# A two-layer hybrid decoder on one core: the opening re-ordered around the raw memory tokens, and the second mixer's end cut into parts

## Chip, cores, metric

One NeuronCore of a Trainium2 chip runs one Bass program (hand-written instruction streams for the five engines, tied together by semaphores). The metric is device time in microseconds of the core. Median before: 1234.83 us of 3 runs (1234.59 to 1236.22).

## The reference, cut to what matters

512 tokens of width 1024 go through two layers; float32 throughout. Each layer adds a mixer, cross attention to 256 memory tokens, and a sparse mixture of experts.

```python
mkv = rmsnorm(mem, mem_norm_g) @ w_mem_kv          # 256x1024 @ 1024x2048, once for both layers
xn  = rmsnorm(h, norm_mix_g[0])                    # layer 0, even mixer: gated MLP half and S5 half
z   = xn @ w_in                                    # 1024 -> 1536; the last 512 columns feed the S5
# S5: lam_bar = exp(lam*step); b_bar = ((lam_bar-1)/lam)*B; a linear scan; y = Re(C x) + D u
# layer 1, odd mixer: z = rmsnorm(h) @ w_in (1024 -> 3592)
hh = rmsnorm(mlstm(q, k, v, i, f), hn_g) * sigmoid(c_o)    # yc, 4 heads
yd = block-sparse causal attention, 4 heads                 # "sparse head" below
h  = h + concatenate([yc, yd]) @ w_out                      # 1024 -> 1024
```

## The kernel before, in words

Matrices live in SBUF as 128-partition blocks; x as four token tiles of 128, transposed into eight blocks of 128 columns. Weights come as panels of 2 MB (all 1024 rows, 512 columns) into two slots W0 and W1 in turn. SP issues each panel when the last result of the slot's previous panel has been filled (`load_panel`, L545).

Two kinds of product. The memory's four panels kv0 to kv3 are plain float32 products (`memory_gemm`, L871; each is two token tiles by eight blocks, and each matmul leaves two records). All layer products are split (`split_gemm`, L813 to L840): for each of the eight steps k, ACT copies the weights' block into a rounded high part (`weights`, L1435), GpSimd subtracts it for the low part (`low_parts`, L674), and TensorE makes three passes for each of four banks (L835). High and low parts have a ring of four. x is split in the same way, ACT the high part (`high_part`, L1427), VectorE the low part (`low_part`, L1933).

PSUM's eight banks go round by a written list (`uses_of_banks`): each use claims its bank when the use before has been copied out. In layer 1 two groups of four banks, G and O, turn separately; the sparse heads' scores (`ms`), turned probabilities (`mt`) and turned gated blocks (`ycT`) share O. The order of work on each engine is the order of the program.

**The opening, before.** SP: memory tokens, the S5 loads (small pieces, L603), kv0 and kv1, x (four quarters, L607), a second copy of B (L610), fifteen small loads (L612), then kv2 and so on. ACT's queue loads the rows of gains; GpSimd's the S5 rows (L649), then it makes the constants, the identity among them, and reports all at once. TensorE turns the gains and S5 rows (`cols`, L849), then the memory, which ACT has squared, and VectorE scaled by its reciprocal root (L1984); VectorE copies the turned blocks times the gain (L1989, L1990). TensorE: kv0, the turned C (`ct`, L882), kv1, kv2, the turned B tables (`bT`, L892), x turned (`mix_norm0`, L813), kv3, the first split panel ev2 (L835), the table product w (L906). VectorE between: S5 angles (L1998 to L2016), powers (from L2019), B and C (to L2038), x's root, ten steps of `combine` for the B tables, x scaled (L2055), nine `combine` for the C powers with x's low parts between (L2044 to L2046). ACT: squares and root of the memory, exponentials and sines (L1504 to L1513), squares of x (L1458) and its root (L1463).

**The second mixer's end, before.** After the last projection (dv, panel od6) TensorE turns the probabilities of sparse head 1 (`moba_turn`, L1368), multiplies head 0 (`moba_out`, L1379), makes head 3's scores (`moba_scores`, L1357), multiplies head 1, turns head 2, turns the gated blocks (L1400), and runs the output panel out10, with the rest of heads 2 and 3 between its steps. VectorE finds each row's maximum (L2585 to L2587), scales the probabilities by the reciprocal sum (`moba_probs`, L2593, L2594), and copies every second bank (L2600); ACT makes the exponentials (L1854) and the other copies (L1862). For the mLSTM half, GpSimd squares all 2048 columns (L765), VectorE sums (L2626), ACT takes the root (L1892), VectorE the reciprocal (L2630), and GpSimd multiplies by it (L768) and by the gate (L769), each in one piece; only then does it make the output panel's low parts. ACT makes that panel's high parts behind head 3's exponentials.

## Time and profile before

| | us |
|---|---|
| median of 3 runs | 1234.83 |
| the profiled execution | 1233.99 |
| its span | 1232.2 |
| TensorE matmul busy | 1163.9 (94%) |
| weight load | 863.5 (70%) |
| VectorE | 716.7 (58%) |
| ScalarE (ACT) | 588.2 (48%) |
| GpSimd (POOL) | 357.5 (29%) |
| DMA, mean over the span | 174 GB/s |
| mean granted TensorE clock | 0.983 of full |

The profile is one execution; its times run from the span's start. "Idle before, releaser" is how long an engine stood still before an instruction and what ended that. Matmul ends are modelled and overlap, so the distance of two starts is their cost. The two stretches that the change touches are 0 to about 122 us and about 795 to 858 us.

### The profile page before, as it was taken

What the parts mean: (1) busy time and instruction counts of PE and PEld (TensorE: products, weight loads), DVE (VectorE), ACT (ScalarE), POOL (GpSimd) and SP (SyncE); (2) the same over time, 40 slices, a digit from 0 to 9 for tenths busy, and PEclk for the clock granted to TensorE, in tenths of its full rate; (3) what the DMA queues carried; (4) which work ended last, traced back from release to release, by engine and by line L of the source; (5) the groups of instructions that cost most, each with busy time, mean ns of one, the idle gap of its engine ahead of it and who ended that gap; (6) DMA issues with size and microseconds to landing.
All of it is one profiled execution on the core that took longest, in us unless ns stands there. A gap on an engine that the chain in (4) does not pass through costs nothing.

```text
span 1232.2 us, 15359 instructions
## 1 busy us (share of the span) xinstructions
PE 1163.9 (94%) x5227; PEld 863.5 (70%) x5227; DVE 716.7 (58%) x1294; ACT 588.2 (48%) x1130; POOL 357.5 (29%) x311
## 2 busy tenths in 40 slices
PE   4999999999999799999899999979999997999996
PEld 2458876788777566666678877757887774666665
DVE  5893443322332688888745992772223326888887
ACT  2453245445634266665535354352465343666661
POOL 2024350564222021113136663253342220211130
PEclk9999999999999899999899999999999998999999
DMA  9532331278102799997232130012321017999963
GB/s 279 150 106 99 40 111 69 70 289 323 69 1 96 299 391 368 391 376 293 72 126 77 69 136 1 2 68 69 137 69 69 1 67 318 380 375 390 379 228 125
DMA packets 77643, 214.92 MB, mean 174 GB/s; under 512 B 23620, under 2 KB 24560, under 8 KB 65272
## 3 DMA queue, kind: packets, MB, share of 16 engines
q1 hardware_dynamic: 64688, 180.22, 39.7%
q0 software_dynamic: 10048, 28.92, 6.4%
q10 hardware_dynamic: 2840, 4.91, 1.1%
q8 instruction: 40, 0.66, 0.2%
q14 instruction: 27, 0.22, 0.1%
HBM read 187.90 MB, written 32.51 MB: 179 GB/s over the span
## 4 chain that ended last, share of the span: by engine, by line
PE 83%; DVE 9%; ACT 3%; issue 2%; DMA 1%; POOL 1%; DVEq 0%; POOLq 0%; ACTq 0%
PE bank L835 39%; PE bank L1183 7%; PE bank L1216 7%; PE bank L1188 6%; PE bank L871 5%; PE bank L1053 2%; PE bank L1075 2%; PE bank L1129 2%; DMA E<-xs,idx 1%; DVE h L2412 1%; PE bank L1102 1%; PE bank L1014 1%; DVE E2r L2373 1%; PE bank L1239 1%; ACT E2r L1736 1%
## 5 line engine op out<-in xcount | busy, mean ns | idle before, releaser
L674 POOL TENSOR_TENSOR wlo<-W,whi 128x512 fp32r<-128x512 f32 x176 | 254.6, 1458 | 451.6 <-ACT whi L1435 431.5
L1435 ACT ACTIVATE whi<-W 128x512 fp32r<-128x512 f32 x176 | 108.1, 633 | 238.4 <-PE bank L835 231.8
L835 PE MATMUL bank<-whi,xTr 128*128 128x512 f32 x480 | 193.1, 402 | 0.9 <-ACT E L1878 0.7
L835 PE MATMUL bank<-wlo,xTr 128*128 128x512 f32 x416 | 162.5, 391 | 0.0
L835 PEld LDWEIGHTS bank<-whi,xTr 128*128 128x128 f32 x480 | 90.6, 189 | 21.8 <-POOL wlo L674 1.7
L835 PE MATMUL bank<-whi,E4r 128*128 128x512 f32 x256 | 99.8, 390 | 0.0
L1188 PE MATMUL bank<-E4r,E1r 128*128 128x512 f32 x360 | 98.5, 422 | 0.0
L1216 PE MATMUL bank<-whi,E2r 128*128 128x512 f32 x256 | 91.2, 418 | 6.7 <-DVE E2r L2373 5.2
L835 PEld LDWEIGHTS bank<-wlo,xTr 128*128 128x128 f32 x416 | 78.6, 189 | 16.6 <-issue 1.2
L1973 DVE TENSOR_TENSOR h<-bank,h 128x512 f32<-128x512 f32 x32 | 21.8, 692 | 115.0 <-PE bank L835 115.0
L1188 PEld LDWEIGHTS bank<-E4r,E1r 128*128 128x128 f32 x360 | 67.6, 188 | 27.0 <-issue 7.4
L707 POOL COPY idx<-slots 128x1 uint32 (+1 forms) x30 | 5.5, 182 | 276.5 <-PE bank L1163 186.0
L1216 PEld LDWEIGHTS bank<-whi,E2r 128*128 128x128 f32 x256 | 49.8, 195 | 24.4 <-DVE E2r L2373 14.2
L835 PE MATMUL bank<-whi,E0r 128*128 128x512 f32 x160 | 63.7, 398 | 0.0
L835 PE MATMUL bank<-whi,E2r 128*128 128x512 f32 x160 | 62.4, 390 | 0.0
L835 PE MATMUL bank<-wlo,E0r 128*128 128x512 f32 x160 | 62.2, 389 | 0.0
L1714 ACT ACTIVATE E4r<-W 128x512 fp32r<-128x512 f32 x56 | 33.2, 626 | 58.7 <-DVE sm L2341 44.5
L871 PE MATMUL bank<-W,E 128*128 128x512 f32 x128 | 57.6, 611 | 3.5 <-DVE E3r L1933 1.9
L1183 PE MATMUL bank<-E 128*128 128x512 f32 x128 | 57.5, 592 | 0.0
L835 PEld LDWEIGHTS bank<-whi,E4r 128*128 128x128 f32 x256 | 48.0, 188 | 10.1
L1216 PE MATMUL bank<-wlo,E2r 128*128 128x512 f32 x128 | 51.4, 402 | 0.0
L1183 PE MATMUL bank<-W,E 128*128 128x512 f32 x112 | 50.5, 594 | 0.7 <-DVE E L2230 0.7
(487 smaller groups left out, 2397.2 us busy)
## 6 DMA issues: line engine op xcount, KB each, us to landing
E<-in_moe_w SPq DMA_DIRECT2D x48, 1024.0 KB, 10.2
W<-in_moe_w SPq DMA_DIRECT2D x32, 1024.0 KB, 10.1
xT<-in_moe_w SPq DMA_DIRECT2D x16, 1024.0 KB, 12.4
W<-in_od_w_in SPq DMA_DIRECT2D x7, 2048.0 KB, 8.5
ybuf<-E SPq DMA_DIRECT2D x26, 512.0 KB, 6.8
ybuf<-memV POOLq DMA_DIRECT2D x12, 1024.0 KB, 19.7
W<-in_w_mem_kv SPq DMA_DIRECT2D x4, 2048.0 KB, 8.1
W<-in_xa_wq SPq DMA_DIRECT2D x4, 2048.0 KB, 8.6
```

Source lines behind the costliest of these rows:

```text
L674: pool.tensor_tensor(wlo[s_ % RING][:, :], slot(name)[:, k, :], whi[s_ % RING][:, :].bitcast(F32), ALU.subtract).then_inc(S["w_lo"], 1)
L835: ins = pe.matmul(bank(u + t)[:, :], a, b, start=(k == 0 and n == 0), stop=(k == KT - 1 and n == 2))
L871: ins = pe.matmul(bank(u)[:, :], memnT[:, k, t * P:(t + 1) * P], slot(f"kv{n}")[:, k, :], start=(k == 0), stop=(k == KT - 1))
L1053: ins = pe.matmul(bank(u)[:, head * NM:(head + 1) * NM], qT[:, k, t * P:(t + 1) * P], memKT[:, k, :], start=(kk == 0), stop=(kk == 1))
L1075: ins = pe.matmul(bank(u)[:, :], memV[:, k, n * XD + d * P:n * XD + (d + 1) * P], pT[:, n, k, :], start=(k == 0), stop=(k == 1))
L1129: ins = pe.matmul(banks[b][:, k * P:(k + 1) * P], xn[:, t, (4 * b + k) * P:(4 * b + k + 1) * P], first1h[:, t, :], start=(t == 0), stop=(t ...
L1183: pe.matmul(banks[2 + par][:, :], xgT[:, k, :], w13s[j][:, :, k, :], start=(k == 0), stop=False)
L1188: ins = pe.matmul(banks[2 + par][:, :], a, b, start=False, stop=(c == SPLIT - 1 and n == 2))
L1216: ins = pe.matmul(banks[5 + half][:, :], a, b[:, :], start=(k == 0 and n == 0), stop=(k == 1 and n == 2))
L1435: act.activation(whi[s_ % RING][:, :], slot(name)[:, k, :], ACT.Copy).then_inc(S["w_hi"], 1)
L1714: act.activation(up_hi[c].rearrange("p (n f) -> p n f", n=2), w13s[nj][:, :, KT - SPLIT + c, :], ACT.Copy)\
L1973: evac(tt(hs, bank(u)[:, :], hs, ALU.add), u)
```

## The change

What it does, in two parts.

*Opening.* The memory tokens are turned raw, as soon as they and their gain row are there; the gain row alone is turned first, in a use of its own (`mg`), behind a first report of the constants that now covers only the identity. VectorE and ACT copy the turned blocks times the gain, two banks each. The reciprocal root of each memory token goes onto the copies of kv0 to kv3 out of their banks (the token is the partition there). The other rows are turned behind the memory. On SP kv0 goes directly behind the memory tokens, ahead of the S5 loads; the small loads go behind kv3. x is turned between kv1 and kv2, its squares on ACT go ahead of the sines, its root and scaling on VectorE ahead of the B tables, its low parts between the first two `combine` steps. kv2, kv3 and the B tables' turn follow. Buffers E1 and E3 change places for the S5 tables, low parts of x and the gated half.

*Second mixer's end.* Squares, gate and normalization on GpSimd are in four pieces each, the gate ahead of the normalization; squares go to E5 in place of E2 and no longer wait for the last projection. The output panel out10 and its twin take the blocks in the order 4, 5, 0, 1, 2, 3, 6, 7 (4 to 7 are sparse heads 0 to 3), and the gated blocks are turned after its first step, each tile behind its own piece. ACT makes the panel's first two high parts ahead of head 3's exponentials and two more behind head 1's high part. Head 3's probabilities are scaled on ACT behind the turned head 2; VectorE only makes the reciprocals, and copies head 0's low part ahead of head 3's maxima.

```diff
-    steps = [("cols", 1), ("memT", 4), ("kv0", 2), ("ct", 2), ("kv1", 2), ("kv2", 2), ("bT", 8), ("mix_norm0", 8),
-             ("kv3", 2), ("s5u", 4), ("w", 8), ...
+    steps = [("mg", 1, (7,)), ("cols", 1), ("memT", 4), ("kv0", 2), ("ct", 2), ("kv1", 2), ("mix_norm0", 8), ("kv2", 2), ("kv3", 2), ("bT", 8),
+             ("s5u", 4), ("w", 8), ...
+        def block_of(name, k):
+            return (4, 5, 0, 1, 2, 3, 6, 7)[k] if name in ("out10", "out11") else k
-        hsq = v3(E[2], 4, 0, 2048)
+        hsq = v3(E5, 4, 0, 2048)
# SP
             sp.dma_start(memtok, ...).then_inc(S["mem_in"], 16)
+            load_panel(0)
             for dst, src in s5_loads:
                 sp.dma_start(dst, src, ...).then_inc(S["s5_in"], 16)
-            load_panel(0)
             load_panel(1)
...
-            for dst, src in small:
-                sp.dma_start(dst, src, ...).then_inc(S["small_in"], 16)
...
                 load_panel(p)
+                if p == pnum["kv3"]:
+                    for dst, src in small:
+                        sp.dma_start(dst, src, ...).then_inc(S["small_in"], 16)
# GpSimd
+            p_(pool.memset(ident[:], 0.0))
+            select(ident[:], 0, [[-1, P]], 1, ALU.not_equal, 1.0)
+            pool.sem_inc(S["consts_ready"], 1)
             for dst, src in lam_loads:
                 pool.dma_start(dst, src).then_inc(S["lam_in"], 16)
...
-            await_filled(pool, first["dv"] + 3)
             taken_all(pool, "num0", 4)
             taken_all(pool, "num1", 4)
-            p_(pool.tensor_tensor(hsq, hh, hh, ALU.mult), "hh_sq")
+            for t in range(TT):
+                p_(pool.tensor_tensor(hsq[:, t, :], hh[:, t, :], hh[:, t, :], ALU.mult), "hh_sq")
+            for t in range(TT):
+                p_(pool.tensor_tensor(hh[:, t, :], hh[:, t, :], SO[:, t, :], ALU.mult))
             pool.wait_ge(S["hh_rstd"], 1)
-            p_(pool.tensor_tensor(h16, h16, drec[:, 0:16]..., ALU.mult))
-            p_(pool.tensor_tensor(hh, hh, SO, ALU.mult), "hh_ready")
+            for t in range(TT):
+                h4 = hh[:, t, :].rearrange("p (n d) -> p n d", n=4)
+                p_(pool.tensor_tensor(h4, h4, drec[:, 4 * t:4 * t + 4]..., ALU.mult), "hh_ready")
             low_parts("out10", "out11")
# TensorE
+            pe.wait_ge(S["mem_in"], 32)
+            u = first["mg"]
+            fill(pe.transpose(bank(u)[:, 0:KT], rows[0:KT, :], ident[0:KT, 0:KT]), u)
             u = first["memT"]
-            for t in range(MT):
-                pe.wait_ge(S["xn_ready"], t + 1)
...
+            u = first["cols"]
+            pe.wait_ge(S["rows_in"], 16 * (len(rows_loads) - 1))
+            pe.wait_ge(S["lam_in"], 16 * len(lam_loads))
...
             memory_gemm(1)
+            transpose_gain_norm("mix_norm0")
             memory_gemm(2)
-            pe.wait_ge(S["s5_bb"], 1)
+            memory_gemm(3)
+            pe.wait_ge(S["s5_tables"], 1)
...
-            transpose_gain_norm("mix_norm0")
-            memory_gemm(3)
             split_gemm(first["s5u"], "ev2", ...)
...
             def moba_turn(n):
-                pe.wait_ge(S["mo_probs"], 4 * (n + 1))
+                if n == 3:
+                    pe.wait_ge(S["last_probs"], TT)
+                else:
+                    pe.wait_ge(S["mo_probs"], 4 * (n + 1))
...
             moba_turn(2)
-            pe.wait_ge(S["hh_ready"], 1)
-            for n in range(4):
+            def gated_turn(n):
                 u = first["ycT"] + n
                 claim(pe, u)
                 for t in range(TT):
+                    pe.wait_ge(S["hh_ready"], t + 1)
                     ins = pe.transpose(bank(u)[:, t * P:(t + 1) * P], hh[:, t, n * P:(n + 1) * P], ident[:])
                 fill(ins, u)
-                           between={} if n else {0: [(moba_out, 2)], 2: [(moba_turn, 3)], 4: [(moba_out, 3)]})
+                           between={} if n else {0: [(gated_turn, k) for k in range(4)], 1: [(moba_out, 2)],
+                                                 2: [(moba_turn, 3)], 4: [(moba_out, 3)]})
# ACT
-            act.wait_ge(S["mem_in"], 16)
+            taken(act, first["mg"])
+            for n in (1, 3):
+                u = first["memT"] + n
+                await_filled(act, u)
+                for kk in range(2):
+                    ins = act.activation(memnT[:, 2 * n + kk, :], ..., ACT.Copy, scale=col("mem_norm_g", 2 * n + kk))
+                evac(ins, u)
...
             act.activation(rho8, are, ACT.Exp, scale=float(LC)).then_inc(S["s5_exp"], 1)
+            squares("mix_norm0")
...
             act.activation(s5cos, ...)
-            squares("mix_norm0")
             root("mix_norm0")
-            copies("kv0", 0, 2, lambda n: memtok[:, n, 0:512])
+            act.wait_ge(S["mem_rstd"], 1)
+            copies("kv0", 0, 2, lambda n: memtok[:, n, 0:512], scale=mem_rstd)
...
+            def moba_probs(n):
+                for t in range(TT):
+                    act.wait_ge(S["sums_ready"], t + 1)
+                    act.activation(pm(n, t), pm(n, t), ACT.Copy, scale=xrec[:, 4 * n + t:4 * n + t + 1])\
+                        .then_inc(S["last_probs"], 1)
...
             moba_high(0)
+            weights("out10", 0, 2)
             moba_exp(3)
-            weights("out10", 0, RING)
             moba_high(1)
+            weights("out10", 2, RING)
             moba_turn(2)
+            moba_probs(3)
# VectorE
-            for t in range(MT):
-                ts(memtok[:, t, :], memtok[:, t, :], rstd[:, 0, t:t + 1], None, ALU.mult).then_inc(S["xn_ready"], 1)
...
-            rstd_of_tokens("mix_norm0")
+            dve.wait_ge(S["std_ready"], v.n["mean_ready"])
+            v(dve.reciprocal(rstd[:, n0, :], std[:, n0, :]))
+            for t in range(TT):
+                ts(h[:, t, :], h[:, t, :], rstd[:, NORMS["mix_norm0"], t:t + 1], None, ALU.mult).then_inc(S["xn_ready"], 1)
             combine(BB1, Fr, B1, Fi, B2)
+            norm("mix_norm0")
             combine(BB2, Fr, B2, Fi, B1, ALU.subtract)
...
-            for t in range(TT):
-                ts(h[:, t, :], ...).then_inc(S["xn_ready"], 1)
             for k in range(LC + 1):
-                if k == 3:
-                    norm("mix_norm0")
                 combine(s5PP[:, :, k, :], Lr[:, :, k], C1, Li[:, :, k], C2)
...
             dve.reciprocal(drec[:, 0:16], dstd[:, 0:16]).then_inc(S["hh_rstd"], 1)
+            moba_low(0)
             moba_max(3)
-            moba_low(0)
-            moba_probs(3)
+            for t in range(TT):
+                taken(dve, first["ms3"] + t)
+                dve.reciprocal(xrec[:, 12 + t:13 + t], xsum[:, 12 + t:13 + t]).then_inc(S["sums_ready"], 1)
             moba_low(1)
```

## Rows read from the trace of the kernel before

**Rows 1.** The page: the chain that ended last, share of the span by engine.
```profile
PE 83%; DVE 9%; ACT 3%; issue 2%; DMA 1%; POOL 1%; DVEq 0%; POOLq 0%; ACTq 0%
```

**Rows 2.** The chain in order of time, opening: start us, us, what.
```profile
20.38 16.04 PE bank L871 x32
37.29 27.48 PE bank L871 x64
87.64 21.82 PE bank L835 x96
```

**Rows 3.** DMA issues, 0 to 90, then the issue lines L545 and L607.
```profile
E<-in_mem SPq DMA_DIRECT2D x1, 1024.0 KB, 5.2
...
L545 SPq DMA_DIRECT2D W<-in_w_mem_kv x2: 508/547/586, 10.1 to 10.7; - x2
DMA to landing us min/median/max: 8.1/10.5/13.0
...
L607 SPq DMA_DIRECT2D h<-in_x x4: 520/599/3644, 11.3 to 16.2; - x4
DMA to landing us min/median/max: 11.2/12.4/13.6
```

**Rows 4.** Timeline, opening: start us, us, engine line op, out<-in xcount [idle before <-releaser].
```profile
20.42 0.19 DVE L1998 TENSOR_TENSOR sm<-sm 128x32 f32<-128x32 f32 x1
...
32.74 0.44 ACT L1510 ACTIVATE memKT<-memKT 128x288 f32<-128x288 f32 x1 [8.20 <-DVE E L2016]
...
33.74 0.46 DVE L2019 TENSOR_TENSOR memKT<-memKT 128x288 f32<-128x288 f32 x1 [1.03 <-ACT memKT L1511]
...
35.32 1.99 ACT L1513 ACTIVATE E<-E,halfpi 128x2048 f32<-128x2048 f32 x1
...
39.17 0.69 DVE L2038 TENSOR_SCALAR E<-bank 128x512 f32<-128x512 f32 x1
...
40.33 1.04 ACT L1458 ACTIVATE memV<-h 128x1024 f32<-128x1024 f32 x1
...
41.48 1.28 ACT L1463 ACT_TABLE_LOAD   x1
...
63.96 2.74 DVE L2055 TENSOR_SCALAR h<-h,rstd 128x1024 f32<-128x1024 f32 x4 [0.15 <-DVE E L2046]
...
68.09 3.66 PE L813 MATMUL bank<-ident,h 128*128 128x128 f32 x32
...
73.67 1.52 PE L871 MATMUL bank<-W,E 128*128 128x512 f32 x3 [1.93 <-DVE E3r L1933]
```

**Rows 5.** Line L612, small loads: ns min/median/max, first and last start us.
```profile
L612 SPq DMA_DIRECT2D rw<-in_moe_w_grp x2: 435/511/587, 18.1 to 30.2; - x2
...
L612 SPq DMA_DIRECT2D gbs<-in_gm_bs x1: 405/405/405, 35.3 to 35.3; - x1
```

**Rows 6.** Timeline, the second mixer's end.
```profile
811.47 23.32 SPq L545 DMA_DIRECT2D W<-in_od_w_out  x2
...
818.44 2.00 PE L1357 MATMUL bank<-E 128*128 128x384 f32 x4 [2.91 <-DVE E L2600]
...
822.37 4.52 POOL L769 TENSOR_TENSOR W<-W,E 128x2048 f32<-128x2048 f32 x1
...
832.39 1.97 PE L1400 MATMUL bank<-ident,W 128*128 128x128 f32 x8 [4.35 <-DVE E L2600]
```

**Rows 7.** The output panel's landing, line L2594, and two groups of the page's costliest.
```profile
W<-in_od_w_out SPq DMA_DIRECT2D x1, 2048.0 KB, 7.8
...
L2594 DVE TENSOR_SCALAR E<-E,st x12: 285/453/3562, 795.1 to 829.8; 128x128 f32<-128x128 f32 x3, 128x256 f32<-128x256 f32 x3, 128x384 f32<-128x384 f32 x3, 128x512 f32<-128x512 f32 x3
...
L674 POOL TENSOR_TENSOR wlo<-W,whi 128x512 fp32r<-128x512 f32 x176 | 254.6, 1458 | 451.6 <-ACT whi L1435 431.5
L1435 ACT ACTIVATE whi<-W 128x512 fp32r<-128x512 f32 x176 | 108.1, 633 | 238.4 <-PE bank L835 231.8
```

**Rows 8.** Windows: us, busy time per engine (x count), granted clock, DMA share, GB/s.
```profile
832.40:838.40 6.00, 6.00 (x21) 5.16 (x22) 2.51 (x4) 1.19 (x2) 0.00 (x0) 0.62 0.48 147
```

More of the change, by code:

```diff
@@ L345, in program @@
         uT = v3(E[4], 4, 0, 2048)
[L346 to L347 removed]
+        yT = v3(E[1], 4, 2048, 4096)
+        sg = v3(E[1], 4, 0, 2048)
         QKT = v3(E[0], 8)
@@ L870, in memory_gemm @@
                     for k in range(KT):
+                        if n == t == 0 and k % 2 == 0:
+                            taken(pe, first["memT"] + k // 2)
                         ins = pe.matmul(bank(u)[:, :], memnT[:, k, t * P:(t + 1) * P], slot(f"kv{n}")[:, k, :],
@@ L1530, in _ @@
                                       accum_out=xmx[:, 4 * t + n:4 * t + n + 1]), "hd_sq")
-            copies("kv3", 0, 2, lambda n: memV[:, n, 512:1024])
+            copies("kv2", 0, 2, lambda n: memV[:, n, 0:512], scale=mem_rstd)
+            weights("ev2", 0, RING)
+            copies("kv3", 0, 2, lambda n: memV[:, n, 512:1024], scale=mem_rstd)
+            for n in range(8):
+                u = first["bT"] + n
+                await_filled(act, u)
+                evac(act.activation(E[3][:, 512 * n:512 * n + 512], bank(u)[:, :], ACT.Copy), u)
             weights_between("ev2", "ev1")
@@ L1973, in add_to_h @@
                         evac(tt(hs, bank(u)[:, :], hs, ALU.add), u)
-            dve.wait_ge(S["consts_ready"], 1)
+            u = first["mg"]
+            await_filled(dve, u)
+            evac(dve.tensor_copy(cols[:, 0:KT], bank(u)[:, 0:KT]), u)
+            taken(dve, u)
+            for n in (0, 2):
+                u = first["memT"] + n
+                await_filled(dve, u)
+                for kk in range(2):
+                    ins = ts(memnT[:, 2 * n + kk, :], bank(u)[:, kk * NM:(kk + 1) * NM], col("mem_norm_g", 2 * n + kk), None,
+                             ALU.mult)
+                evac(ins, u)
             u = first["cols"]
```

110 lines of the change are left out of this document (52 added, 58 removed), and 2 rows, old and new, of the table steps.

## The prediction, made before the changed kernel ran

> **What bounds the kernel now.** I read the page first. The chain that ended last is TensorE for 83% of the span [rows 1], so a microsecond comes back only where TensorE stands still or where work ahead of its first matmul shrinks. Next the chain in order of time: the first panel of the memory (32 matmul records) starts at 20.38, 64 more follow from 37.29, and the even mixer's first split panel runs from 87.64 for 21.82, to 109.5 [rows 2]. So the chip spends 20.4 us before its first large matmul. Then the timeline for what TensorE waits for: 1.93 us before the fourth memory panel, for a bank [rows 4]; at the end of the second mixer 2.91 us before a sparse head's scores, then 4.35 us before the last two gated blocks are turned, both for VectorE's copy at L2600 [rows 6]. These are the places that the change touches. Last, the DMA rows, because the opening is a race of transfers [rows 3].
>
> **The opening: a new start for TensorE.** Now the memory is squared, rooted and scaled before it is turned, and its panel is queued behind seven small S5 loads. After the change the raw tokens are turned and the factor goes onto the copies out of the banks. The tokens land 5.2 us after an issue at once, near 6. Thirty-two transposes take 3.66 at full speed [rows 4], so the 16 of the memory take 1.8, or 3.7 at half. With the new gain transpose and the last copy out, about 11.1. The panel goes second on the queue: 1 MB lands in 5.2, 2 MB in 8.1 [rows 3], so 3 MB land about 11 after the first issue, at 11.8. First matmul 11.8 in place of 20.38. That would be 8.6 us, if nothing else held it.
>
> **The opening: what is late next.** x is now normalized and turned after the second memory panel, where it was behind the third. TensorE is there at 11.8 + 16.04 + 0.87 (the C transposes, from 36.42 to 37.29) + 13.74 (half of 27.48) = 42.5, and would be done with x at 46.1. The other engines: x is issued from 11.3 to 16.2 and lands 11.2 to 13.6 later, so its last quarter is there near 28 [rows 3]. The queue carries the same bytes ahead of it afterwards; the gaps between the small S5 loads may fall in behind the 2 MB, and I take 27.5. Four squares of 1.04 (the fourth begins at 40.33) end at 31.8. The S5 angles are ready on VectorE 12.3 after they begin (20.42 to 32.74) [rows 4]; now they need the S5 loads. Those filled the queue from the memory's landing, near 6, to 12.5 or so (the panel issued behind them at 10.1 still landed 8.1 later), so they come some 7 us after the panel, near 19, and the angles at 31.4: level with the squares. A table load of 1.28 and two small sines (about 0.9) give 34.0. VectorE then needs what it did from 33.74 to 39.86 (6.1): 40.1; ACT's large sines, 1.99 and as much again, a table load and a root end at 39.5, beside it. The reciprocal and four scalings of 2.74 end at 43.1, and the transposes, of which the first column block needs all four tiles, at 46.6 [rows 4]. Hence 0.5 us of waiting in a place where there was none, and this chain, not the first matmul, sets the gain.
>
> Behind it TensorE has two panels (27.5), the B transposes (3.6), and the split panel (22.0 with its first step): 99.7, against 109.5 [rows 2]. The old 1.93 us wait goes, because the low parts of x come before the long S5 tables. Before, the first tables kept VectorE from the root near 43 to just ahead of the scaling at 63.96, 21 us; now they take those 21 and x's eight low parts (some 6) behind 43.1, so 70, and TensorE wants them at 74.1. The second set is nine steps like the eight of the first, so ready by 90, before 99. The wait of some 1 us behind the memory keys' scaling stays as it is. **Opening: -9.8 us**, bounds -7 and -12.
>
> Costed at nothing, and their cover: the fifteen small loads, moved from ahead of the third panel to behind the fourth's issue. Their issues now run from 18.1 to 35.8 [rows 5], 17.7 us of SP. They would run from 42 to 60; the next load on SP, the split panel, may start when the third panel is used up, at 60.4. It lands at 68.5 and TensorE wants its first parts at 77.7, so 7 us of cover remain after one high and one low part of 0.63 and 1.46 [rows 7]. The transposes of gains and S5 rows come from the other queues behind memory's, while the panel lands. The swap of buffers 1 and 3 moves no work. The memory copies with a scale are as long as those without. The ident matrix first on GpSimd costs the S5 row loads 0.7 us, and nothing waits for them before 10. The copies of memory to SBUF are split between VectorE and ACT, under the landing.
>
> **The second mixer's end.** From the last projection (811.3, where the output panel is issued) to the end of the first output step with the gated blocks turned (838.4) it takes 27.1. Part of that is clock: in 832.4 to 838.4, after the long wait, the granted clock is 0.62 [rows 8], so much of it on the lower of 1.2 and 2.4 GHz; of the 6.00 busy there 1.97 is turning [rows 6], so the step took 4.0 where an eighth of 21.82 is 2.7.
>
> What the parts remove: GpSimd starts its squares when the heads are stored (near 802) and not at 811.5, and its product with the gate no longer stands behind the root. Quarters of 4.52/4 = 1.13 at the slowest [rows 6]: squares and gates end by 811, so VectorE's sum is not late and the 2.91 us wait goes. The four last scalings go from VectorE, where one of L2594's took 3.56 at a median of 0.45 [rows 7], to ACT; the 4.35 us wait behind them goes too. What takes their place is a panel. ACT now makes two high parts before the last head's exponentials, and these need the output panel, which is issued at 811.47 [rows 6] and lands 7.8 later [rows 7], at 819.3. Until then ACT stands, with the exponentials, the second head's high part and the copies of the turned head queued behind. Then 2 x 0.63, a table load of 1.28: exponentials from 821.9; the third frees the bank for the third head's turn about 1.8 later (three like ACT's 128x512 of 0.63 would take 1.9, and two of these are shorter), at 823.7. The turn (ten transposes at 3.66/32 each, 1.2) ends at 824.9. GpSimd's first low part is ready at 819.9 + 1.46 = 821.4, its gated quarters before that. So the first output step runs 824.9 to 828.2 (between 2.7 and 4.0), the gated blocks (1.97) to 830.1. **End: 838.4 - 830.1 = -8.3 us**, bounds -4 (below) and -11 (no panel wait: the turn then follows the second head's product at 819, and the first step starts near 821.4).
>
> The trace has no quarters of GpSimd beside VectorE's scalings of the head before (807 to 809). The near row is L2594's spread [rows 7]: 3.56 beside one whole GpSimd piece. With quarters of 1.13 each scaling may wait for one: at most 4 x 1.13 = 4.5 us on VectorE, nothing if they miss each other. I take 2.7; the scores then end near 820.6, still before 821.9. The panel wait is its cover.
>
> The Trainium skill, "SBUF — State Buffer", section "Who interferes with whom", says that a GpSimd operation and a VectorE one in a two-port mode, or one with two SBUF inputs, exclude each other for the whole instruction. It speaks against starting GpSimd's work under VectorE's scalings; the row of 3.56 agrees, and by the rule four scalings wait for one quarter each, as in the bound above, so the sum stands. It also favours quarters over one piece of 4.52.
>
> **Sum.** 1233.99 (the profiled execution, with 1.8 outside its span of 1232.2) - 9.8 - 8.3 = 1215.9. The median of the three is 0.8 above the profiled one, so about 1216.5. Behind both places TensorE is without long waits, and what follows should shift whole.
>
> **Rivals.** (1) Both gains, larger: x lands by 26, no wait at x, the first panel runs warm (its 32 took 16.04 where later ones take 13.7), and the exponentials do not wait: 11.5 + 11 = 22.5, 1211.5. For it: holes in the early transfers; against: the panel's 7.8. 15%. (2) x or the S5 loads come 4.5 us later than I take, since many small packets now stand behind a full queue: -5.3 and -8.3, 1220.4 (or 1221 by the median). 14%. (3) GpSimd stays the bound at the end: its quarters and VectorE's work lengthen each other, and its first low part comes at 828.3, as now (826.9 + 1.3): the end gives 4, 1220.2. 12%. (4) The change does not do what it says for the opening: the shift is given back at a later wait, for the S5 tables or ev panels; only the end counts, 1225.7. 6%. (5) Slower: TensorE's order is fixed, so at x's transposes it stands with the third panel already landed, where it used to have two panels of work. It decides when the scaled x is ready after 61 (43.1 + 9.8 + 8.3); at 65 it costs 4 net, 1238. That needs the x or S5 loads 20 us late. 3%. The forecast itself has 50%, with 1213 to 1219.
>
> **How the numbers follow.** A measurement of this kernel tells about 0.2%, 2.5 us, from no change. Rivals 1 to 4 and the forecast all lie beyond that below: 0.95 with a little of 5's neighbourhood taken off; within it 0.02; slower 0.03. The range takes in 1 to 3 and the bounds -7-4 and -12-11 in good part: 1210 to 1223.5.
>
> **What would show it.** First matmul of the memory panel near 12; x's transposes ending near 46.6, with a wait of 0 to 2 us for the scaling; no wait at the fourth panel; the split panel ending near 100. At the end: ACT idle until the output panel lands, about 8 us after its issue; L2594's wait gone; the first output step 13.5 us after the last projection. Wrong if TensorE waits over 4 us at x, if the split panel waits for its load, or if the distance from the last projection to the first output step stays above 20 us.

## The result, and the profile of the changed kernel

The changed kernel takes **1217.99 us** (median of 4 runs, 1217.23 to 1220.30) against 1235.53 for the kernel before in its 4 runs (1234.59 to 1237.11): a ratio of 0.986, 95% interval 0.9842 to 0.9878, or 17.5 us less. The profiled execution took 1217.23 with a span of 1215.5, at a mean granted clock of 0.984; the one of before took 1233.99 with 1232.2, at 0.983. The two spans differ by 16.7 us, and this is what the rows below account for.

The page: TensorE's busy row, and the chain that ended last by engine.

```profile
PE 1162.6 (96%) x5228; PEld 863.1 (71%) x5228; DVE 718.2 (59%) x1285; ACT 592.1 (49%) x1138; POOL 362.9 (30%) x320
...
PE 83%; DVE 8%; ACT 3%; DMA 2%; issue 2%; SPq 1%; DVEq 0%; POOLq 0%; POOL 0%; ACTq 0%
```

Beside [rows 1] the shares hardly differ: 17 us of 1215 is work that came off the front and a pause that came out of the middle, not another bound. Where it came from stands in the chain in order of time (start us, us, what), first the opening, then the second mixer's end.

```profile
16.85 11.95 DMA h<-in_x
...
28.82 1.20 ACT memV L1482 x3
...
33.10 1.28 ACT L1543
...
41.96 2.75 DVE h L2102 x4
44.76 3.38 PE bank L823 x29
48.14 27.47 PE bank L882 x64
...
79.11 21.82 PE bank L845 x96
...
802.94 7.66 DMA W<-in_od_w_out
...
810.62 1.15 ACT whi L1459 x2
...
811.79 1.28 ACT L1890
...
813.69 1.62 PE bank L1382 x10
815.30 4.08 PE bank L845 x12
819.38 1.75 PE bank L1415 x16
...
835.37 2.16 PE bank L1393 x8
```

**The opening.** The first split panel ends at 79.11 + 21.82 = 100.9, before at 109.5 [rows 2]: 8.5 us. Its chain no longer begins with TensorE's first panel. It begins with the landing of x, then come the squares, the table load, the S5 sines, VectorE's scaling of x, and only from 44.76 TensorE. Read from the memory panel alone (20.38 before, 12.03 now) one would have said 8.35 and been right by accident: that panel is not on this chain.

**The end.** The output panel is issued at 802.94, lands 7.66 later, is copied twice, then a table load, then the first exponentials: the same pieces that the prediction lists. The gated blocks are turned at 819.38 + 1.75 = 821.1, which is 18.2 behind the issue. Before, the issue was at 811.47 [rows 6] and the same point at 838.4 [rows 8]: 26.9. So 8.7 us.

The issue itself moved from 811.47 to 802.94, 8.5 us: all that the opening gave is still there 700 us later, and nothing was given back in between. 8.5 + 8.7 = 17.2; the spans differ by 16.7. The stretch behind this place took 377.5 before and 378.0 now, and in the fourteen profiles of this case it takes 377.2 to 380.0, so the 0.5 lies inside the scatter.

What TensorE waits for, from the views of 0 to 125 and of 780 to 850 (engine line, releaser: us in total, times, longest).

```profile
PE bank L882 <- DMA W<-in_w_mem_kv: 1.5, 1, 1.5
PE bank L823 <- DVE h L2102: 1.5, 4, 0.5
...
PE bank L1382 <- ACT E L1890: 2.3, 1, 2.3
```

The 2.91 and 4.35 of [rows 6] are gone, as is the 1.93 of [rows 4]. New are 1.5 at x (four tiles, each a little late) and 2.3 at the turn of head 2, the third head.

The timeline (start us, us, engine line operation [idle before <- releaser]), opening and end.

```profile
3.26 8.22 SPq L608 DMA_DIRECT2D E<-in_s_c_re  x1
...
12.03 15.70 PE L882 MATMUL bank<-W,E 128*128 128x512 f32 x32 [1.48 <-DMA W<-in_w_mem_kv]
...
15.19 2.21 SPq L611 DMA_DIRECT2D h<-in_x  x4
...
28.82 1.06 ACT L1482 ACTIVATE memV<-h 128x1024 f32<-128x1024 f32 x1 [9.02 <-DMA h<-in_x]
...
69.68 2.19 ACT L1459 ACTIVATE whi<-W 128x512 fp32r<-128x512 f32 x4 [7.08 <-DMA W<-in_ev_w_in]
...
78.86 0.47 PE L845 MATMUL bank<-xTr,whi 128*128 128x512 f32 x1
...
793.47 4.39 POOL L772 TENSOR_TENSOR E<-W 128x512 f32<-128x512 f32 x4 [9.71 <-DVE W L2627]
...
797.94 5.40 POOL L774 TENSOR_TENSOR W<-W,E 128x512 f32<-128x512 f32 x4
...
800.85 1.34 DVE L2645 TENSOR_SCALAR E<-E,st 128x384 f32<-128x384 f32 x1
...
807.64 4.39 POOL L778 TENSOR_TENSOR W<-W,st 128x512 f32<-128x512 f32 x4 [4.31 <-DVE st L2681]
```

SP stood 8.22 us on one S5 issue behind the first 2 MB, so x was issued from 15.19, where it was issued from 11.30 before. Yet it landed at the same time: its last quarter, issued at 16.80, was there at 28.82; before, issued at 16.19, it took 12.8 and was there at 29.0. The same bytes stand ahead of it in both. The small loads, now behind the fourth panel's issue, cost nothing: the split panel's copies run from 69.68, wanted at 78.86. At the end GpSimd has squares and gate done by 803.3. Its quarters of the gate (5.40 for four) and VectorE's scalings of head 2 do lie on each other: the scalings of 256, 384 and 512 columns take 1.33, 1.34 and 1.32, where the median of such a line was 0.45 [rows 7].

### The profile page after: what moved, and what is told of

It reads as the page before. It is cut to its first block, busy times and chain, and to the rows that moved or that the text cites. A ratio compares the mean times of both kernels' runs of the same rounds, so it can differ in the third digit from the quotient of the medians.

```text
span 1215.5 us, 15377 instructions
## 1 busy us (share of the span) xinstructions
PE 1162.6 (96%) x5228; PEld 863.1 (71%) x5228; DVE 718.2 (59%) x1285; ACT 592.1 (49%) x1138; POOL 362.9 (30%) x320
## 4 chain that ended last, share of the span: by engine, by line
PE 83%; DVE 8%; ACT 3%; DMA 2%; issue 2%; SPq 1%; DVEq 0%; POOLq 0%; POOL 0%; ACTq 0%
PE bank L845 39%; PE bank L1194 7%; PE bank L1227 7%; PE bank L1199 6%; PE bank L1064 2%; PE bank L1086 2%; PE bank L882 2%; PE bank L1140 2%; DVE h L2463 1%; PE bank L1113 1%; PE bank L1025 1%; SPq L608 1%; DVE E2r L2424 1%; DMA h<-in_x 1%; PE bank L1250 1%
## 5 line engine op out<-in xcount | busy, mean ns | idle before, releaser
L1227 PEld LDWEIGHTS bank<-whi,E2r 128*128 128x128 f32 x256 | 49.8, 195 | 24.6 <-DVE E2r L2424 14.6
L845 PEld LDWEIGHTS bank<-whi,E4r 128*128 128x128 f32 x256 | 48.0, 188 | 10.1
## 6 DMA issues: line engine op xcount, KB each, us to landing
E<-in_moe_w SPq DMA_DIRECT2D x48, 1024.0 KB, 10.1
```

What stands on the lines that cost most here:

```text
L845: ins = pe.matmul(bank(u + t)[:, :], a, b, start=(k == 0 and n == 0), stop=(k == KT - 1 and n == 2))
L1227: ins = pe.matmul(banks[5 + half][:, :], a, b[:, :], start=(k == 0 and n == 0), stop=(k == 1 and n == 2))
```

## The experiments

Several executions of one kernel showed first that medians separate less here than the prediction's 0.2%. The kernel before stays within 3.5 us over the 13 runs of the first session (in the third one run stood at 1243.8), the variants of the changed one spread over 3 to 12. So each experiment was read by distances inside its profile. Two of them recur. The *opening* is read at the end of the first split panel (109.5 before, 100.9 changed). **D** is the distance from the issue of the output panel to the end of the last head's product, the last place that all orders share: 811.47 to 854.75 = 43.3 before, 802.94 to 837.52 = 34.6 changed (chain rows above). D depends on the clock too: both of these have a first output step at the lower level (4.01 and 4.08), while mixer_only, kv0_behind_s5, x_before_kv1 and small_early, whose end is the changed kernel's code, have steps of 2.73 to 2.78 and a D of 33.1 to 33.3. A variant of the end is therefore compared with 34.6 where its first step ran slow and with 33.1 to 33.3 where it did not. "Before" means the kernel before on the same chip: 1235.78, 1235.59 and 1236.09 in the three sessions.

**opening_only**: the mixer's hunks undone, the opening's kept.

> The changed kernel with the second mixer's end as before (GpSimd in whole pieces, block order 0 to 7, gated blocks turned ahead of the first output step, head 3 scaled on VectorE, no high part ahead of its exponentials). If the two parts are independent: split panel ends at 100.9 as in the changed kernel, the end of the mixer takes 27.1 from the output panel's issue to the first step with the gated blocks turned, time 1235.5 - 8.5 = 1227.0. Rival (a part pays only beside the other, or is given back later): over 1229 or under 1225.

Measured: 1228.47 (10 runs, 1225.16 to 1234.12), ratio 0.9942 [0.9924, 0.9960]: -7.3. In its profile x is there at 30.2, x is turned by 49.5 and the split panel ends at 102.3: -7.2, against the changed kernel's -8.5. The scatter has one source that can be read. Windows of its profile (us, busy us per engine, granted clock, DMA share, GB/s), over the small transposes and the first products behind the split panel:

```profile
118.00:122.00 4.00, 3.59 (x38) 3.23 (x36) 1.28 (x2) 1.19 (x2) 0.00 (x0) 1.00 0.35 40
122.00:126.00 4.00, 4.00 (x23) 4.00 (x22) 0.00 (x0) 0.00 (x0) 0.00 (x0) 0.54 0.76 101
126.00:130.00 4.00, 4.00 (x21) 4.00 (x20) 0.00 (x0) 0.00 (x0) 0.00 (x0) 0.50 0.62 84
...
134.00:138.00 4.00, 4.00 (x15) 3.17 (x14) 0.00 (x0) 0.63 (x1) 0.47 (x1) 0.75 0.00 0
```

and the same code in the changed kernel's profile, then a window on its first output step:

```profile
122.00:126.00 4.00, 4.00 (x37) 4.00 (x37) 0.00 (x0) 0.00 (x0) 0.00 (x0) 1.00 0.74 99
...
815.00:817.00 2.00, 2.00 (x7) 1.62 (x6) 1.42 (x3) 2.00 (x6) 0.69 (x1) 0.50 0.00 0
```

In one execution TensorE gets the lower of its two levels (1.2 and 2.4 GHz) for some 12 us, in the other not; 23 matmuls pass in 4 us where 37 did. Ahead of the fall stands the same row of short transposes in both. TensorE was busy 3.59 of 4 us in the window before it; the kernel before shows 3.59 in one of its windows here too, and so does block_order in the same window of the same opening, and both keep full speed. The fall cost 6.3 us: from the end of the split panel to the issue of the output panel it took 708.3, where the kernels before and after took 702.0. So in this profile the issue came only 0.9 before its old place (810.58), and the gain of the opening had gone to the clock and not to a wait. The runs bear it out: opening_only's three runs above 1233 had a mean granted clock of 0.978, those near 1225 had 0.983.

**mixer_only**: the opening's hunks undone.

> The changed kernel with the opening as before. Independent parts: split panel ends at 109.5, the mixer's end takes 18.2 in place of 27.1, time 1235.5 - 8.9 = 1226.6. Rival as for the other half: over 1229 or under 1225.

Measured: 1225.62 (4 runs, 1223.51 to 1228.79), 0.9928 [0.9907, 0.9950]: -10.2. Its first split panel runs from 87.64 for 21.82, exactly [rows 2]. Its chain at the end (start us, us, what):

```profile
811.04 7.75 DMA W<-in_od_w_out
...
823.24 2.78 PE bank L842 x12
...
841.98 2.16 PE bank L1389 x8
```

D = 844.14 - 811.04 = 33.1, against 34.6: here the first step takes 2.78, not 4.08. So the end is worth 43.3 - 33.1 = 10.2 where the first step runs at full speed, and 8.7 where the lower level falls on it (0.50 in the window above). The 8.7 compares two slow steps (4.01 and 4.08) and is what the change itself gave; the other 1.5 is clock. By medians -7.3 and -10.2 make -17.5, which is the whole change, though each median is known only to 2 or 3 us; by distances it is 7.2 + 10.2 = 17.4 against 8.5 + 8.7 = 17.2. **The halves add up; nothing shows either living off the other.** Rival (4) is settled by the changed kernel itself, whose output panel is issued the full 8.5 earlier.

**kv0_behind_s5**: the first memory panel behind the S5 loads again.

```diff
-            load_panel(0)
             for dst, src in s5_loads: sp.dma_start(...)
+            load_panel(0)
             load_panel(1)
```

> The changed kernel, the first memory panel queued behind the seven S5 loads again. Theory (the opening's end is the later of TensorE's own work and of x's chain): first matmul at 18.3 instead of 12.0; TensorE's own work is then the later, 18.3 + 15.7 + 0.9 + 13.8 = 48.7, x turned at 52.2 instead of 48.1, so +4, about 1222, and no wait left at x. Rival (the gain is the first panel's place and nothing else): +6.3, 1224.3. Rival (x's chain alone sets it): 0.

Measured: 1223.77 (4 runs, 1218.96 to 1226.98), 0.9892 [0.9860, 0.9924]. Chain:

```profile
18.86 16.32 PE bank L882 x32
...
49.79 3.49 PE bank L823 x32
...
84.25 21.82 PE bank L845 x96
```

And the start of the squares of x in its timeline:

```profile
30.21 1.06 ACT L1482 ACTIVATE memV<-h 128x1024 f32<-128x1024 f32 x1 [11.04 <-DMA h<-in_x]
```

The first panel starts 6.8 later than in the changed kernel, the split panel ends at 106.1, 5.1 later, and TensorE has no wait at x any more. So there are two chains side by side in the opening. TensorE's own, without a wait at x, would have x turned 3.5 after the second panel's end, 42.3 in the changed kernel (28.44 + 13.90 in its timeline), so at 45.8. x's own has it turned at 48.1, 2.3 later. TensorE's was delayed by 49.8 - 42.3 = 7.5 (6.8 in the start, the rest in a slower first panel), and 7.5 - 2.3 = 5.2 should arrive: measured, 5.1. (The theory had put 4, from a start of 18.3 and a first panel of 15.7; the median, 5.8 above the changed kernel's, does not tell it from the rival's 6.3, since two of the four runs had a clock of 0.981 or less and the profiled one shows a fall at 126 to 140.) This run also answers whether SP's 8.22 us made x late. Here the same issue stood 3.44, x was issued from 11.38, and yet it was there only at 30.2. The place of x in the queue of bytes, not the time of its issue, is what its landing follows.

The later experiments kept this opening and show x's chain again. In the nine profiles with it (the changed kernel twice, opening_only, exp_first, exp_three, probs_vector, block_order, small_early, pool_whole) x was there at 28.75 to 30.78, and the last run of its transposes (29 of them) began 15.94 to 15.96 after that in every one, whether TensorE's first panel took 14.00, 15.70 or 16.8. The split panel ended at 100.9 to 104.6.

**x_before_kv1**: if x's chain is the longer one, x should be loaded sooner.

```diff
+            for k in range(TT): sp.dma_start(h[:, k, :], ...)
             load_panel(1)
-            for k in range(TT): sp.dma_start(h[:, k, :], ...)
```

> The changed kernel, x issued ahead of the second memory panel. Theory (x's landing at 28.8 starts the chain squares, sines, scaling that TensorE waits for): x lands near 23.6, the squares end by 28.1, the angles at 29.3 take over as the late one, scaled x ready at 39.8 instead of 44.7; TensorE then sets the end, with the second panel landing near 28.8 (up to 0.5 late): x turned at 46.4 instead of 48.1, -1.7, about 1216.3. Rival (TensorE's order sets it, x is never late): 0, or +0.5 for the panel.

Measured: 1219.71 (4 runs, 1212.65 to 1224.25), 0.9875 [0.9827, 0.9922]. A miss. x was there at 23.3, 5.5 sooner, and x's turn ended at 48.92, 0.8 later than in the changed kernel:

```profile
16.84 12.85 DMA W<-in_w_mem_kv
...
29.73 15.70 PE bank L882 x32
...
48.92 27.47 PE bank L882 x64
```

The second panel now landed 12.85 after its issue, at 29.7 (the theory had 28.8), and TensorE stood 2.8 before it. It then took 15.70 where it takes 13.90 without such a wait ahead: the granted clock was 0.85 from 29.7 to 31.7 and 0.50 from 31.7 to 33.7. I had counted the queue's order and not its bytes: whichever of x and the panel goes last lands near 29 to 30, and either is wanted before. The order between them moves the wait; without the 1.8 of clock the turn would have ended near 47.1, about 1 sooner than in the changed kernel (an estimate).

**x_first_exp_three**: the fuller attempt. x goes second, the S5 tables behind both panels, with the low log-step row on GpSimd's queue; VectorE scales x ahead of the S5 work; TensorE takes the C transposes behind both panels; and the end is that of exp_three below.

```diff
             load_panel(0)
-            for dst, src in s5_loads: sp.dma_start(...)
-            load_panel(1)
             for k in range(TT): sp.dma_start(h[:, k, :], ...)
+            load_panel(1)
+            for dst, src in s5_loads: sp.dma_start(...)
...
-("kv0", 2), ("ct", 2), ("kv1", 2), ("mix_norm0", 8)
+("kv0", 2), ("kv1", 2), ("ct", 2), ("mix_norm0", 8)
```

> Both readings put to use: exp_three's order at the end, and an opening in which x goes directly behind the first memory panel, the second panel next, the big S5 loads last (the step sizes ride on GpSimd's queue), C turned behind the second panel, x scaled ahead of B and C on VectorE. Theory (the queue's bytes up to x set the opening): x lands near 18 to 20, TensorE never waits for it; x turned at 12.0 + 15.7 + 13.8 + 0.9 + 3.5 = 45.9 instead of 48.1, the end 2.4 shorter: about 4.6 below the changed kernel, 1213.5. Rival (S5 loads last make C or the B tables late): the first split panel or C's turn waits, gain of the opening 0 or less, 1215.5.

Measured: 1220.17 (6 runs, 1214.36 to 1224.52), 0.9873 [0.9845, 0.9901]. A miss by 6.7 by the median; the profiled execution had a span of 1212.6, the shortest of all profiled, at a clock of 0.989. Timeline:

```profile
12.12 0.41 PE L871 MATMUL bank<-ident,junk 108*128 108x108 f32 x1 [2.43 <-DMA sm<-in_s_log_step]
...
43.62 3.66 PE L824 MATMUL bank<-ident,h 128*128 128x128 f32 x32
...
48.00 1.52 PE L883 MATMUL bank<-W,E 128*128 128x512 f32 x3 [0.72 <-DVE E1r L1980]
```

x's chain is out of the way: scaled from 34.9, no wait at x, and both panels run in 29.93 from 12.98. Yet the next panel starts at 48.0, as before, and the split panel ends at 101.0. TensorE started 1 us later (the rows' transpose waited for the moved log step), and between the turn's end at 47.3 and the panel a bank waited 0.7 for VectorE's copies. So **TensorE's own work from 12 on is nearly the whole of it**: 12 + 14.0 to 15.7 for the first panel + 1.0 + 13.9 + 3.5 is 44.4 to 46.1, against 48.1. By this estimate the order of the loads has at most 2 to 4 us left to give in this opening, and each wait that I took away made another of about that size.

**small_early**: the fifteen small loads back ahead of the third panel.

> The changed kernel with the fifteen small loads ahead of the third memory panel again. Theory (costed at nothing in either place): they hold SP from 18.7 to 36.4, the third panel is issued then instead of at 27.8 and lands at 44.5, before TensorE wants it at 48.1: x turned at 48.1, split panel's end at 100.9, as in the changed kernel. Rival (they had to move, else the third panel is late): a wait before the third panel, x's stage plus 1 or more.

Measured: 1220.81 (4 runs, 1216.41 to 1224.20), 0.9883 [0.9849, 0.9916]; but x turned by 48.2 and the split panel's end at 101.0, both within 0.1 of the changed kernel. The move of the small loads is worth nothing, as the prediction costed it. The median's +2.8 has no place in this profile, which is that of the fastest of the four runs.

**exp_first**: ACT makes the last head's exponentials first, then all parts of the panel.

```diff
             moba_high(0)
-            weights("out10", 0, 2)
             moba_exp(3)
+            weights("out10", 0, RING)
             moba_high(1)
```

> The changed kernel with head 3's four exponentials ahead of all of the output panel's high parts, as before. Measured by D, the time from the output panel's issue to the end of head 3's product (34.6 in the changed kernel, 43.3 before). Theory (the panel's landing only moves the wait; maxima at +6.3 to +9.6 after the issue pace the exponentials otherwise): the turn of head 2 comes 1.8 earlier, but the first high part is made near +10.9 and the low part at +12.2, so the first output step starts where it does now: D 34.6, or up to 1.5 less where the granted clock does not fall. Rival (parts ahead of the exponentials are what brings the gain): D 37 to 38.

Measured: 1217.21 (4 runs, 1215.74 to 1222.70), 0.9861 [0.9834, 0.9888]. Chain:

```profile
811.00 1.09 PE bank L1382 x10
...
814.94 4.58 PE bank L845 x12
```

The wait moved. The turn of head 2 comes 8.5 behind the issue and not 10.8, but TensorE then stands 2.85, while ACT makes the high part (from 812.81) and GpSimd the low part (from 813.57), and takes 4.58 for the first step: D = 837.65 - 802.50 = 35.2, no gain. With a first step at full speed it would be near 33.4 (an estimate: 35.2 less 4.58 - 2.76), close to the 33.1 to 33.3 of the changed order.

**exp_three**: three of the four exponentials first (those free the turn), one high part, the fourth, the next.

```diff
             moba_high(0)
-            weights("out10", 0, 2)
-            moba_exp(3)
+            moba_exp(3, 0, 3)
+            weights("out10", 0, 1)
+            moba_exp(3, 3, 4)
+            weights("out10", 1, 2)
             moba_high(1)
```

> The changed kernel, ACT making three of head 3's exponentials, then one high part, then the fourth, then the second. Theory (now the landing at +7.7, two copies, a table load and three exponentials stand in a row): the three exponentials end at +9.0, the turn at +10.2, the low part at +10.9, so the first step starts 1.4 earlier; D 33.2, and 31.9 if the granted clock stays up. Rival (the low part on GpSimd or the turn's bank is the late one anyway): D 34.6.

Measured: 1217.05 (4 runs, 1211.92 to 1217.59), 0.9836 [0.9811, 0.9860]. Chain:

```profile
811.42 1.09 PE bank L1382 x10
...
814.01 3.01 PE bank L845 x12
...
833.00 2.16 PE bank L1393 x8
```

D = 835.16 - 802.95 = 32.2, 2.4 less than changed (and 32.2 again in x_first_exp_three). Of these, 1.1 are the first step at 3.01 in place of 4.08, which is clock, and the rest is the turn under the panel's landing. Against the 33.1 to 33.3 of the changed order at full speed, 0.9 to 1.1 is left. By the median it is 0.9 below the changed kernel, with intervals that lie on each other: shorter in its place, not shown faster as a whole.

**probs_vector**: the last head is scaled by VectorE again and not by ACT.

```diff
-                dve.reciprocal(xrec[:, 12 + t:13 + t], xsum[:, 12 + t:13 + t]).then_inc(S["sums_ready"], 1)
+                v(dve.reciprocal(xrec[:, 12 + t:13 + t], xsum[:, 12 + t:13 + t]))
+                ts(pm(3, t), pm(3, t), xrec[:, 12 + t:13 + t], None, ALU.mult).then_inc(S["last_probs"], 1)
...
-            moba_probs(3)
```

> The changed kernel with head 3's probabilities scaled on VectorE, as before, instead of ACT. Theory (what hurt before was the scaling standing behind whole GpSimd pieces with the turned head's copy behind it; GpSimd now only has two low parts there): VectorE is at most 2 us later with head 1's low part, inside the first step's 4 us: D 34.6 to 35.6. Rival (the move to ACT is what removed the 4.35 us wait): D 38 to 39.

Measured: 1217.96 (4 runs, 1216.62 to 1219.81), 0.9852 [0.9835, 0.9868]; D = 839.96 - 806.71 = 33.3, with the first step at 2.79. That is the D of mixer_only (33.1). With the rest of the change in place, moving these four scalings to ACT is worth nothing that D shows. They take 0.70, 0.36, 0.42 and 0.49 on VectorE, where the first of them took 3.56 before [rows 7]. The 4.35 us wait behind them [rows 6] goes without the move.

**pool_whole**: GpSimd's squares, gate and factor in whole pieces, begun as soon as in the changed kernel.

```diff
-            for t in range(TT):
-                p_(pool.tensor_tensor(hsq[:, t, :], hh[:, t, :], hh[:, t, :], ALU.mult), "hh_sq")
+            p_(pool.tensor_tensor(hsq, hh, hh, ALU.mult), "hh_sq")
```

> The changed kernel with GpSimd's squares, gate and normalization in one piece each, in the new order and place. Theory (the output panel's landing covers them): VectorE's scalings of head 2 stand behind the gate's whole piece, about as long as now behind four quarters; root and reciprocal within 1 us of now, normalization done by +9, first low part at once. D (output panel's issue to the end of head 3's product) 34.6, or 33.3 if the granted clock stays up. Rival (the quarters bring the gain): D 37 or more.

Measured: 1219.79 (4 runs, 1215.39 to 1222.61), 0.9873 [0.9842, 0.9903]. GpSimd's timeline:

```profile
793.14 3.60 POOL L771 TENSOR_TENSOR E<-W 128x2048 f32<-128x2048 f32 x1 [9.71 <-DVE W L2623]
...
807.12 3.61 POOL L775 TENSOR_TENSOR W<-W,st 128x2048 f32<-128x2048 f32 x1 [5.70 <-DVE st L2677]
```

D = 835.60 - 802.58 = 33.0. A whole piece takes 3.6 and four quarters 4.4, and neither is on the path: the D is that of mixer_only. Whole pieces that start at 793 do as well as quarters. VectorE's scalings of head 2 beside the gate's whole piece take 3.02, 0.35, 0.42 and 0.49, together 4.3, beside its quarters 4.5: one long wait or several short ones.

**block_order**: the output steps in the order 0 to 7 again, gated blocks turned ahead of the first.

> The changed kernel with the blocks in order 0 to 7 again and the gated blocks turned ahead of the first output step. Theory (the first step on a sparse head's block covers the copies of head 2, its scaling and the gated blocks' high parts on ACT): the gated blocks' last three banks wait for the copies at +15, block 0's parts are there at +17.8, so the first step starts 5 later than now with 1.8 of turning done: D 37.5 to 38.5. Rival (the order is indifferent once the pieces are quarters): D 34.6.

Measured: 1220.93 (4 runs, 1218.86 to 1227.25), 0.9892 [0.9860, 0.9924]. Chain:

```profile
820.28 0.70 DVE E5r L1978
...
821.03 3.02 PE bank L845 x12
```

The first step starts 17.7 behind the issue, not 12.4. It waits for the first gated block's low part on VectorE (L1978), which waits for its high part on ACT, and that stands behind head 3's scalings (817.8 to 819.8). D = 840.41 - 803.34 = 37.1, 2.5 more than in the changed kernel and 4 more than in the variants whose first step, like this one, ran at full speed (33.0 to 33.3). The order of the blocks, 4 and 5 first with the gated blocks turned behind them, is what lets TensorE work while ACT and VectorE finish the rest. Of the end's parts that I undid one by one, this is the one that costs something.

**after_again**: the changed kernel unchanged, beside the last experiments.

> The changed kernel itself, on the same chip as the version above, because executions of one kernel differ by some us where the granted clock falls at other places. Expected 1218 with a spread of a few us; the distances in its trace (x turned at 48.1, split panel's end 100.9, D 34.6) the same within 1.5 us.

Measured: 1217.53 (6 runs, 1215.01 to 1223.34), 0.9844 [0.9819, 0.9869]. The profiled execution was its longest, 1223.34, and shows how one and the same kernel comes to 6 us more:

```profile
43.92 2.75 DVE h L2102 x4
46.72 5.05 PE bank L823 x29
```

x was there at 30.8 and not at 28.8 (2.0 later), its scaling began 2.0 later, and the turn behind it took 5.05, not 3.38: 3.6 us in the opening alone, and 2.0 more behind the end. D is 841.61 - 806.88 = 34.7, as expected; the opening's two distances were expected within 1.5 and missed that (51.8 for 48.1, 104.6 for 100.9). So a landing that differs by 2 us between executions goes through to the split panel's end one to one, and can take the clock with it. The same turn took 3.38 in the six profiles of this opening where TensorE's longest wait before it was 0.3 to 1.6, and 5.05, 4.72 and 6.09 in the three where it had stood 2.5, 2.5 and 2.9 (after_again, pool_whole, probs_vector); from 48 to 50 the granted clock here was 0.50.

## Why the prediction was right

The forecast was 1216.5, by the sum 1215.9 in the profiled execution; measured were 1217.99 and 1217.23, inside its own 1213 to 1219. The mechanism held, but part of the closeness is luck: the opening gave 1.3 less than the sum has and the end 0.4 more, and in three of the nine profiles with this opening (after_again, probs_vector, pool_whole) it gave 4.9, 4.9 and 6.8, below the bound of 7. Step by step:

- **First matmul, 11.8**: 12.03. Right, with the wait for the panel's landing as the prediction had it.
- **x lands at 27.5**: 28.8. This is the mis-sized term of the opening. The prediction read the old landing as "near 28" out of the shortest and the longest of four times [rows 3]; the last quarter's own time was 12.8 from an issue at 16.2, so 29.0. It then took 0.5 off for holes that would fall away, and x landed 0.2 sooner. It also did not foresee that SP would stand 8.22 us on an S5 issue, but this did not make x late: in kv0_behind_s5 SP stood 3.44 and x landed at 30.2. The rest of the chain held. Squares end 33.1 (31.8), scaled 44.7 (43.1), turned 48.1 (46.6), split panel's end 100.9 (99.7): the 1.3 of the landing, give or take 0.3 on the way. The gain is 8.5, not 9.8.
- **Angles level with the squares, at 31.4**: they were ready at 29.3, and no S5 wait stands on the chain. VectorE waited 6.1 until 35.40 for ACT's sines, which came behind the squares. Right in its result, too late in its estimate.
- **"This chain, not the first matmul, sets the gain"**: right, and kv0_behind_s5 measures it: TensorE's own chain ends 2.3 sooner (the prediction had 0.5), so the two are nearly level. x_before_kv1 and x_first_exp_three add what the prediction did not see, that moving x alone is no way out.
- **No wait at the fourth panel, small loads free, 7 us of cover**: right. The copies began at 69.7 (68.5), with 9.2 to the first matmul that wants them. Among the things costed at nothing one was not quite: the copies of the memory panels out of their banks take 0.69 on ACT with the scale and took 0.60 without (0.09 each, off the chain).
- **The end, 18.6 from issue to turned gated blocks**: 18.2. Landing 7.66 (7.8), two high parts, a table load, exponentials from 813.1, 10.1 behind the issue (10.4): as written. The turn then began at 813.7, behind the first exponential, which frees its first bank, and not behind the third, and ended at 815.3, 12.4 behind the issue (13.4). Of this 1.0 the first step took back 0.8: 4.08 at the lower level where the prediction took 3.3. The gain is 8.7, not 8.3, and 10.2 where the clock stays up. The end thus came near the sum by two errors against each other.
- **Scalings of head 2 lengthened by 2.7 in all**: about 2.9, covered by the panel wait. The longer three take 0.83 to 0.98 more than their own 0.35, 0.42 and 0.49, and a quarter of the gate took 1.35 beside them (1.13 in the prediction). The Trainium skill, "SBUF — State Buffer", "Who interferes with whom", has a GpSimd and such a VectorE operation exclude each other for a whole instruction. The rows agree: each scaling lengthens by most of one quarter. What the prediction drew from it, that the rule favours quarters, made no difference: pool_whole has whole pieces, the scalings lengthen by 2.7 in all, and D is 33.0.
- **Four scalings to ACT remove the 4.35 us wait**: the wait went, but probs_vector shows that the move was not what removed it. The prediction gave the gain to the move, and this step of it failed, without a cost in the sum. block_order shows what 4.0 of the end's 10.2 belongs to. The early start of GpSimd is the part that was not undone alone; that the rest belongs to it is argued from the chain before, where its squares (811.5 to 815.1) and VectorE's sum of them stood on the path, and not shown.

The rivals. (1) needed x by 26 and no panel wait; neither. (2) needed x 4.5 later; it was 1.3. (3), GpSimd as the bound, fell: its last quarter ended at 812.0, while TensorE wanted the gated blocks at 819.4. (4) is excluded by the issue of the output panel, 8.5 earlier, and (5) never came near: the scaled x was there at 44.7, not 61.

Not settled: why an execution falls to the lower level at 122 to 136 and another does not. It was seen in the profiles of opening_only and kv0_behind_s5 (there at 126 to 140), and in no other, the changed kernel's two among them. I tried nothing that would control it.

## What to carry to other kernels

When a load is moved forward, ask which chain is next to it, and count the bytes in front of both: here two transfers of equal need shared one queue, and neither of the two other orders that I tried gained anything, in part because a wait at the other place cost clock. Where a pause in the middle is cut into parts, undo the parts one by one: here the order in which the consumer takes the blocks carried gain, while the size of the pieces and the engine of the last scaling carried none. And compare variants of 1 to 3 us by a distance inside the profile, from one shared event to another, since their medians differ by as much from clock and landings alone. Read the granted clock beside the distance: the same code had a D of 33.1 and of 34.7.

## What the runs showed of the hardware that was not expected

- **The variants scatter more than the kernel before.** 1225.16 to 1234.12 over 10 runs of opening_only, 1212.65 to 1224.25 over 4 of x_before_kv1 (mean granted clock 0.989 and 0.980), against 1233.81 to 1237.31 over 13 of the kernel before beside them (in all its runs one stood apart, 1243.82 at a clock of 0.976). The longer time goes with the lower mean clock. The fall of 122 to 136 (clock 0.50, about 6 us) is one place of it.
- **The same wait costs the clock in one execution and not in the other.** Behind a wait of 2.3 us at the turn the first output step took 4.08 in the changed kernel and 2.78 in mixer_only, whose granted clock was 1.00 there; pool_whole had 2.5 and took 2.76, after_again 2.5 and took 3.89. In exp_first it was 4.58 behind 2.85. So the wait alone does not decide it.
- **An issue on SP can stand 8.2 us.** The third issue behind the first 2 MB panel stood 8.17 to 8.35 in the ten profiles with this order of loads, and the same issue 3.44 to 3.60 in the three where only the memory tokens' 1 MB was ahead. Everything behind it on SP is issued later for it, but x did not land later: its landing followed the bytes ahead of it. That the queue was full is my reading; no row names it.
- **The landing of one load differs by 2 us between executions.** The last quarter of x was there at 28.75 to 30.78 in nine profiles of one opening, and the split panel's end moved with it.
